# Splitting the merged result beside its neighbours: the seam between a merge and the output stage of a hybrid backbone step

## The reference, cut to what matters

```
h = modulate(x, norm_mix, shift1, scale1)              # shift, scale, gate = silu(cond) @ w_ada + b_ada
z, xbc, dt, q, k, v, pin, gate_logits = split(h @ w_in)
y_ssd  = ssd_mixer(z, xbc, dt)                          # state space branch
o_attn = gqa_attend(rope(rms_norm(q)), rope(rms_norm(k)), v)
o_pool = multiscale_pool(pin)
g = sigmoid(gate_logits)
merged = g[0]*(y_ssd @ w_ssd_out) + g[1]*(o_attn @ w_attn_out) + g[2]*(o_pool @ w_pool_out)
x = x + gate1 * (merged @ w_out)                        # the output stage
x = x + gate2 * moe_ffn(modulate(x, norm_ffn, shift2, scale2))
y = rms_norm(x)
```

## Time and profile before

| | |
|---|---|
| median of three runs | 2137.48 us (2137.0 to 2142.66) |
| the profiled execution | 2140.71 us, span of its instructions 2138.8 us |
| mean granted TensorE clock | 0.977 |
| TensorE busy | 2023.4 us, 95% of the span |
| VectorE, ScalarE busy | 1408.9 us (66%), 952.5 us (45%) |
| memory traffic | 460.97 MB, mean 216 GB/s |

### The profile page before, as it was taken

How to read it: one execution, slowest core, us unless ns; L and a number is a source line. 1 busy time by engine, 2 the same in 40 slices (tenths; PEclk the granted TensorE clock), 3 DMA queues, 4 the chain that set the end, 5 groups by cost and what they waited for, 6 DMA issues and landing times. The chain is left out here.

```text
span 2138.8 us, 28019 instructions
## 1 busy us (share of the span) xinstructions
PE 2023.4 (95%) x10972; PEld 1743.6 (82%) x10972; DVE 1408.9 (66%) x2046; ACT 952.5 (45%) x1364; POOL 7.8 (0%) x12
## 2 busy tenths in 40 slices
PE   7899999989999999999999969996999999999995
PEld 2299988977888899999999968886877877887774
DVE  1467675526454287774777744355889889889996
ACT  1333565321444232223322233343767667667773
POOL 0000000000000000000000000000000000000000
PEclk9999999999999999999999989997999999999998
DMA  9934343433434456554455566541989989999992
GB/s 370 394 122 146 111 133 105 128 106 148 141 112 148 177 194 209 208 186 164 140 205 197 204 204 238 197 158 49 335 306 354 316 311 338 312 315 340 350 347 103
DMA packets 133513, 460.97 MB, mean 216 GB/s; under 512 B 17568, under 2 KB 23520, under 8 KB 133248
## 3 DMA queue, kind: packets, MB, share of 16 engines
q1 hardware_dynamic: 133376, 459.12, 61.2%
HBM read 455.06 MB, written 4.00 MB: 215 GB/s over the span
## 5 line engine op out<-in xcount | busy, mean ns | idle before, releaser
L185 DVE TENSOR_TENSOR wlo<-raw,whi 128x1024 fp32r<-128x1024 f32 x640 | 779.8, 1224 | 527.6 <-ACT whi L179 506.0
L179 ACT ACTIVATE whi<-raw 128x1024 fp32r<-128x1024 f32 x640 | 678.7, 1060 | 852.1 <-PE bank L207 551.8
L205 PE MATMUL bank<-hhi,whi 128*128 128x384 f32 x1664 | 571.1, 343 | 8.6 <-DVE wlo L185 3.4
L207 PE MATMUL bank<-hhi,wlo 128*128 128x384 f32 x1664 | 560.3, 337 | 0.0
L206 PE MATMUL bank<-hlo,whi 128*128 128x384 f32 x1664 | 560.3, 337 | 0.0
L205 PEld LDWEIGHTS bank<-hhi,whi 128*128 128x128 f32 x1664 | 315.1, 189 | 38.8 <-issue 23.6
L206 PEld LDWEIGHTS bank<-hlo,whi 128*128 128x128 f32 x1664 | 315.4, 190 | 0.8
L207 PEld LDWEIGHTS bank<-hhi,wlo 128*128 128x128 f32 x1664 | 314.9, 189 | 0.0
L2171 PE MATMUL bank<-whi,group_hi 128*128 128x512 f32 x512 | 204.2, 399 | 7.5 <-DVE wlo L185 6.1
L2173 PE MATMUL bank<-wlo,group_hi 128*128 128x512 f32 x512 | 201.5, 394 | 0.0
L2172 PE MATMUL bank<-whi,group_lo 128*128 128x512 f32 x512 | 201.1, 393 | 0.0
(11 more groups left out here) (323 smaller groups left out, 2081.1 us busy)
## 6 DMA issues: line engine op xcount, KB each, us to landing
raw<-in_dense SPq DMA_DIRECT2D x448, 512.0 KB, 4.7
raw<-in_moe SPq DMA_DIRECT2D x384, 512.0 KB, 5.1
merged<-in_x SPq DMA_DIRECT2D x8, 768.0 KB, 7.6
cs_rows_bc<-cs_rows SPq DMA_DIRECT2D x8, 768.0 KB, 5.2
out_y<-y_normed SPq DMA_DIRECT2D x3, 768.0 KB, 4.9
shift_rows<-cs_rows SPq DMA_DIRECT2D x2, 1024.0 KB, 10.1
pool_w_sb<-in_pool_w SPq DMA_DIRECT2D x1, 1024.0 KB, 7.3
pool_inv_count<-in_pool_inv SPq DMA_DIRECT2D x1, 768.0 KB, 7.0
```

The costliest lines, as they stand in the source:

```text
L179: self.nc.scalar.activation(self.whi[:, k % W, :], self.raw[:, n % R, :], ACT.Copy).then_inc(self.hi_done, 1)
L185: self.nc.vector.tensor_tensor(self.wlo[:, k % W, :], self.raw[:, n % R, :], self.whi[:, k % W, :].bitcast(F32), ALU.subtract).then_inc(se ...
L205: self.nc.tensor.matmul(out, self.whi[:, s, c], xhi[:, k, :], start=(k == 0), stop=False)
L207: last = self.nc.tensor.matmul(out, self.wlo[:, s, c], xhi[:, k, :], start=False, stop=(k == blocks - 1))
```

## The change

1. `split_merged_phase` and its barrier are gone. A new `Split` makes the parts in eight pieces of two blocks. In the third merge ScalarE makes high parts 0 to 3 behind the last tanh, and only then the last weight split; VectorE makes low parts 0 to 2 ahead of the last gate product, and part 3 and the last weight split behind the last bias add. Parts 4 to 7 of both stand at the head of the output stage.
2. TensorE waits, block pair by block pair in the first two own tiles of the output stage, for the low part that it reads (`ready`).
3. The four reloads of x go into SyncE's queue behind the loads issued at tiles 1, 8, 16 and 24 of the output stage, each with its own semaphore, and VectorE waits for one at the first block of each round.
4. Attention's generators of TensorE, ScalarE and VectorE begin two steps later (on VectorE 13 empty steps ahead of the head norms instead of 11), and tile 13 takes two steps. The wait in `HeadsSplit` stands two steps later.

```
-def merge_phase(N, ohi, olo, first, name, side=None, lead=0, parts=None):
+def merge_phase(N, ohi, olo, first, name, side=None, lead=0, parts=None, split=None):
 # ScalarE
-                N.act_hi(act, i, body, t)
+                last = split and i == iters - 1 and o == 11
+                if not last:
+                    N.act_hi(act, i, body, t)
...
+            if split:
+                split.high(act, 0, 4)
+                N.act_hi(act, i, body, t)
 # VectorE
+            if split:
+                nc.vector.sem_inc(split.s_ready, 1)
+                split.low(dve, 0, 3)
             merge(*before)
             ada_add(N, dve, iters - 1)
...
+            if split:
+                nc.vector.sem_inc(split.s_ready, 1)
+                split.low(dve, 3, 4)
+                N.dve_lo(dve, i, body, t)
 # Attention
-        return (2, 2, 1)[tile % 3] if tile < 13 else 1
+        return (2, 2, 1)[tile % 3] if tile < 14 else 1
 # Attention.pe, Attention.act
+        for _ in range(2):
+            yield
 # Attention.dve
-        for _ in range(11):
+        for _ in range(13):
             yield
 # HeadsSplit.pe
-        yield
+        for _ in range(3):
+            yield
         pe.wait_ge(self.s_lo, 8)
+X_AGAIN = (1, 8, 16, 24)
+class Split:
+    def high(self, act, lo, hi):
+        for u in range(lo, hi):
+            act.wait_ge(self.s_ready, 1 if u < KB // 2 - 1 else 2)
+            N.nc.scalar.activation(N.hhi[:, 2 * u:2 * u + 2, :], N.merged[:, 2 * u:2 * u + 2, :], ACT.Copy, scale=0.5)\
+                .then_inc(self.s_hi, 1)
+    def low(self, dve, lo, hi):
+        for u in range(lo, hi):
+            dve.wait_ge(self.s_hi, u + 1)
+            N.nc.vector.scalar_tensor_tensor(out=N.hlo[:, 2 * u:2 * u + 2, :], in0=N.merged[:, 2 * u:2 * u + 2, :], scalar=0.5,
+                                             in1=N.hhi[:, 2 * u:2 * u + 2, :].bitcast(F32), op0=ALU.mult, op1=ALU.subtract)\
+                .then_inc(self.s_lo, 1)
+    def x_again(self, sp, b):
+        sp.wait_ge(self.s_lo, 2 * b + 2)
+        sp.dma_start(self.N.merged[:, 4 * b:4 * b + 4, :], self.N.io.x[:, 4 * b:4 * b + 4, :]).then_inc(self.x_in[b], 16)
 # out_phase, SyncE
                 N.load(sp, N.tile0 + s + R)
+                if s in X_AGAIN:
+                    split.x_again(sp, X_AGAIN.index(s))
 # out_phase, ScalarE and VectorE, at their heads
+            split.high(act, 4, KB // 2)
+            split.low(dve, 4, KB // 2)
 # out_phase, VectorE, ahead of the add of x
+                        if m % 4 == 0:
+                            dve.wait_ge(split.x_in[i], 16)
 # out_phase, TensorE
-                        N.pe_tile(pe, i, body, t, B[o // 2 % 2][:, 0:T], N.hhi, N.hlo, 8 * (o % 2), KB)
+                        N.pe_tile(pe, i, body, t, B[o // 2 % 2][:, 0:T], N.hhi, N.hlo, 8 * (o % 2), KB, None,
+                                  lambda k: pe.wait_ge(split.s_lo, k // 2 + 1) if i == 0 and o < 2 and k % 2 == 0 else None)
```

More of the change, by code:

```diff
@@ L194, in dve_lo, with pe_tile @@
         self.split_low(dve, self.own(self.tile(i, body, t)) + LEAD)
-    def pe_tile(self, pe, i, body, t, out, xhi, xlo, k0, blocks, between=None):
+    def pe_tile(self, pe, i, body, t, out, xhi, xlo, k0, blocks, between=None, ready=None):
         n = self.own(self.tile(i, body, t))
@@ L204, in pe_tile @@
                 next(between, None)
+            if ready:
+                ready(k)
             self.nc.tensor.matmul(out, self.whi[:, s, c], xhi[:, k, :], start=(k == 0), stop=False)
@@ L1098, in _ @@
                     continue
-                N.dve_lo(dve, i, body, t)
+                last = split and i == iters - 1 and o == 11
+                if not last:
+                    N.dve_lo(dve, i, body, t)
                 if before:
@@ L1534, in pe, with __init__ @@
             yield
[L1537 to L1560, removed]
-                sp.dma_start(N.merged[:, 4 * b:4 * b + 4, :], N.io.x[:, 4 * b:4 * b + 4, :]).then_inc(x_in, 16)
-            sp.wait_ge(x_in, 64)
+X_AGAIN = (1, 8, 16, 24)
+class Split:
+    def __init__(self, N):
+        self.N = N
+        self.s_ready, self.s_hi, self.s_lo = N.sem("merged_ready"), N.sem("merged_hi"), N.sem("merged_lo")
+        self.x_in = [N.sem(f"x_again{b}") for b in range(4)]
+    def high(self, act, lo, hi):
+        N = self.N
+        for u in range(lo, hi):
[3 more added lines that the diff above has]
+    def low(self, dve, lo, hi):
+        N = self.N
+        for u in range(lo, hi):
[6 more added lines that the diff above has]
+        sp.dma_start(self.N.merged[:, 4 * b:4 * b + 4, :], self.N.io.x[:, 4 * b:4 * b + 4, :]).then_inc(self.x_in[b], 16)
 def rank_steps(st, nc, v, ahead, after, before, rank):
@@ L1663, in __init__, with out_phase @@
          self.s_gc, self.s_zero, self.s_sq, self.s_sum, self.s_y, self.s_out, self.s_diag, self.s_root) = [sem("ff_" + n) for n in names]
-def out_phase(N, E):
+def out_phase(N, E, split):
     nc, io, xt, B, sem = N.nc, N.io, N.merged, N.bank, N.sem
@@ L1708, in _ @@
             sp.wait_ge(s_ld, 80)
+            for b in range(4):
+                sp.wait_ge(split.x_in[b], 16)
         @block.gpsimd
@@ L2266, in build @@
     pooling = Pooling(N)
-    merge_phase(N, N.S["hi"], N.S["lo"], False, "pool", pooling, 2 * POOL_BLOCKS, parts="dve")
+    split = Split(N)
+    merge_phase(N, N.S["hi"], N.S["lo"], False, "pool", pooling, 2 * POOL_BLOCKS, parts="dve", split=split)
     N.at = N.arena
-    split_merged_phase(N)
     E = Experts(N)
-    out_phase(N, E)
+    out_phase(N, E, split)
     expert_rounds(N, E)
```

## The result

The changed kernel takes 2129.44 us, the median of five runs (2124.84 to 2130.04), beside 2137.89 of the kernel before on the same chip: a ratio of the single runs of 0.994, interval 0.9927 to 0.9954. By the ratio that is 12.8 us, by the two medians 8.45, where 19.75 were forecast. The profiled execution took 2129.99 us with a span of 2128.2, 10.6 less than the 2138.8 of before.

What follows compares the result with a forecast made beforehand. TensorE is busy for 95% of the span, so gains must come from its standstills or half clock. Terms: -13.45 + 2.7 - 5.4 - 3.6 = -19.75 us, from 2137.48 to a forecast median of 2118; range 2111.5 to 2126.

Steps and rivals of the forecast that it cites:

- Item 1: Seam between third merge and output stage: moving the split into the merge tail starts TensorE 13.45 us earlier.
- Item 2: Clock at the new seam: still half, so no gain taken; bound up to 2.6 us if at full clock.
- Item 3: Four reloads of x among the output stage's weight loads: +2.7 us in sum, bounds 0 to 6.
- Step (a): First reload of x: needed some 9 us after issue, lands in 4.3 to 6.8 us like before, costs nothing.
- Step (b): Second reload, ahead of tile 15's load in the output stage: delays the chain to TensorE's first fold, +2.0 us.
- Step (c): Third reload, output stage: delays tile 23, so the router's constants come 0.7 us later, +0.7.
- Step (d): Fourth reload, next group of the output stage: queue half empty and TensorE doesn't wait for it, costs nothing.
- reloads bite harder: Rival, chance 0.20: output-stage stalls lower the clock, or a third reload is felt; +3 to +4 us, 2121.5.
- Item 4: First merge, attention's first step one tile later: shorter wait for cached v, no half clock; -5.4 us, bounds -2 to -7.
- the 3 us that I had named as a sign of being wrong: First merge: new waits of attention's units summing to over 3 us would show the forecast wrong.
- a rival at 0.08: Attention gives its gain back: softmax units meet other tiles, 0.25 us more per unit, 6 in all; 2123.7, chance 0.08.
- Item 5: Second merge, heads' wait one tile later: 1.93 us idle and 1.7 of half clock saved, -3.6 us, bounds -1.9 to -4.

Runs made afterwards that it cites:

- the seven traces named above: Output stage up to `pick`: three traces with the reloads where the change puts them, 212.2 us on average; four traces without them, 206.0 us.
- attention's part alone: Kernel before with only attention's steps moved one tile later; 2142.13 us beside 2144.07, ratio 0.999.
- the changed kernel again: The changed kernel measured and profiled once more, without any edit; 2129.55 us, ratio 0.9935 to the kernel before.
- The shift by three tiles: Kernel before with attention's steps moved three tiles later instead of one; 2135.86 us beside 2145.76, ratio 0.996.
- late reloads and attention by three: Changed kernel with reloads 2 to 4 behind tiles 11, 19 and 27 and attention three tiles later instead of one; 2122.11 us beside 2145.06, ratio 0.9897.

## Why the prediction was right and wrong

**Item 1, the seam: right.** 13.45 us forecast and 13.45 measured, with the gap of 2.81 us ended by the barrier. VectorE's timeline has the order that the sum assumed: bias add, fourth low part, weight's low part.

```profile
1241.25 0.17 DVE L292 TENSOR_TENSOR mods<-bank,b_ada_sb 128x8 f32<-128x8 f32 x1 [0.53 <-PE bank L269]
1241.39 0.96 DVE L1582 SCALAR_TENSOR_TENSOR hlo<-merged,hhi 128x768 fp32r<-128x768 f32 x1
1242.26 1.22 DVE L185 TENSOR_TENSOR wlo<-raw,whi 128x1024 fp32r<-128x1024 f32 x1
```

The low part took 0.96 us, not 0.85 to 0.9. The waits ahead of every second block cost nothing; TensorE's rows show no idle time there.

**Item 2, the clock: right.** The two conditioning tiles took 4.03 us as before, so taking no gain was the right choice over the 2.6 us of its bound, and the clock had fallen ahead of TensorE's new start, as the item argued.

**Item 3, the reloads: mechanism right, size wrong.** Step (a) holds: the reloads land as fast as in the earlier trace rows, and VectorE's first add doesn't wait for one.

```profile
DMA to landing us min/median/max: 5.1/5.6/6.8
```

Step (b) said +2.0 us at the first fold; it waits 2.00. Step (c) said +0.7 at the constants; it was 0.42 (1.91 for 1.49). Step (d) said nothing; the third fold waits 1.71 where it had waited 1.04. All waits of the stage rose by 2.8 us in sum (23.13 to 25.94), near the 2.7 of the forecast. What failed is the clock: I put it in the bounds and not in the sum, with the argument that the 1.49 us stop had lowered nothing. In this trace each stop near 2 us was followed by a drop, and a third drop came behind the fold at 1330.38, which had waited only 0.90. Three at 1.7 are 5.1, and 2.8 + 5.1 = 7.9 for the 7.6 measured. Over the seven traces named above the term is 6.2 us, with 2.7 drops a trace where the kernels without the reloads have 0.5; so about 1.4 of the 7.6 us are chance, and the term of +2.7 lacked some 3.5 us for the clock. Even my bound of 6 was too low for this pair, because I allowed two drops. The rival "reloads bite harder" said +3 to +4; it named the mechanism and was short as well.

**Item 4, attention: wrong.** The wait for v went fully here, because the drop at 444 had delayed TensorE on its way there; without that drop it was 0.62 and 0.45 (attention's part alone, the changed kernel again), near the 0.9 of the forecast. In sum TensorE's idle time in the first merge fell from 9.64 to 6.36 us, so 3.3 were saved and not the 4.93 of the wait, because new stops came: 2.06 us at the rotary step for 0.71 before, and 3.0 for exponentials for 0.7. The new part of both is 3.65 us, more than the 3 us that I had named as a sign of being wrong. And drops went from one to three: +3.4 instead of -1.4. One of these three, at 444, isn't the change's: the 1.84 us stop at the head of the merge is the same in both traces, and in the trace of before it brought no drop. The step that failed is "so the lockstep is the same one tile later". It is the same against the steps of the side job, but not against the tiles: units and tiles go by threes, and a shift by one changes which unit meets which tile. I had this as a rival at 0.08 and with a spread over all 24 units; it came as two single stops. The shift by three tiles shows what the item was worth with the relation kept: -7.9 us, more than the 5.4 forecast, whose bound was -7.

**Item 5, heads: right, with some luck in the number.** 3.79 us measured, 3.6 forecast. Of it 1.7 is the drop behind the stop, which two of the four traces with that stop have and two have not. In this pair the drop is gone, and the window from 755 to 758 has its full clock back (the earlier trace rows had 0.51):

```profile
755.00:758.00 3.00, 3.00 (x19) 3.00 (x18) 3.00 (x5) 1.44 (x2) 0.00 (x0) 1.00 0.53 175
```

**The sum.** Item 4 is off by 6.2 us and item 3 by 4.9; 2.0 us came back elsewhere, nearly all of it in stretches that the change doesn't touch, which is luck. The two rivals that came true came together, and I had weighed them as if only one could. The time of 2129.44 lies above my range, which ends at 2126. The ratio of 0.994, put on the 2137.48 that the forecast started from, gives 2124.7, inside the range and near its end. So the range was about wide enough for the total, but not because its terms were right.

**What stays open.** Why a drop follows one stop and not another of the same length isn't settled (last section). The small gain of moving the shift rows is seen in one trace only. What the order of the loads at the head of the stage costs, where SyncE stands for the store of the shift rows (1.6 us in the changed kernel, 3.8 in the one with late reloads and attention by three), wasn't tried apart.

## What to carry to other kernels

Count a stop of TensorE as its length and, by the share of such stops that brought a drop (the counts stand in the next section), the 1.7 us of the drop, in the sum and not in the bounds. When side work is moved along a stream of tiles of several kinds, move it by a whole period of both patterns; one tile off turned a gain of 8 us into none. A transfer put into the queue of the weights is paid in full by the one tile behind it, so put it where that tile has slack. Look also at what is loaded only once in the same stretch: a gain ahead of a stretch whose DMA engines are full can be lost in it, as the wait of 4.05 to 4.73 us here shows. And before you read a term off one pair of traces, look at the same stretch in every trace whose code for it is the same; here such stretches differed by up to 3.9 us.

## What the runs showed of the hardware

I had not expected drops of the clock behind stops so short. Of stops of about 2 us some brought one (1.93 in the earlier trace rows, 2.00 and 1.91 in the output stage of the changed kernel, 1.91 at 747.92 with attention by three), and others not: 1.84 at 444.50 before, 1.91 at 545.04 with attention by three, 2.10 at the constants when the changed kernel ran again. Counted over all 14 traces from 440 to 1425 us, leaving out the stop of 16 us of the old seam, a drop begins in a stop or within 4 us behind it for 15 of 15 stops of 2.3 to 4.9 us, for 17 of 33 of 1.6 to 2.3, and for 7 of 38 of 1.2 to 1.6. The same stop in the same code brings one in some executions only: the 1.84 us at the head of the first merge in 5 of 14, the heads' 1.91 to 1.93 us in 2 of 4. A stop of 0.90 at 1330.38, with the fold's matmuls of few columns behind it, brought one; of 0.94 at the same fold before, none. A stop of 0.74 behind the 16 fold matmuls of one column, at the head of the third merge, has one in the traces before and after (959.84, 955.96), and none when the changed kernel ran again. The Trainium skill (TensorE: Matmul & The Clock Gate, HAM oscillation) speaks of long idle gaps only; here the measured rows decide, and they show drops behind stops of 2 us and less.

The drop can be kept away: with products that nobody reads in the 2.8 us gap the clock was 1.00 on both sides of it in all four kernels that had them, and the four conditioning products took 1.05 us where they had taken 1.92.
